# A second-matrix pair more per group by seven products, and the MLP's row factor moved onto the residual

## The reference, cut to what matters

```
y = h * rsqrt(mean(h*h) + 1e-6) * gain
h = h + square(relu(y @ w_up)) @ w_down      # w_up 1024 x 4096, w_down 4096 x 1024, float32
```

## Time and profile before

| | us |
|---|---|
| median of 3 runs (1189.15 to 1189.55) | 1189.25 |
| the profiled execution's own time | 1188.87 |
| its span, first to last instruction | 1187.1 |
| PE / PE weight load busy | 1176.7 / 1126.4 |
| DVE / ACT / POOL busy | 957.6 / 740.0 / 118.2 |
| MLP of layer 0: first matmul of the first pair to the end | 250.9 to 597.5 |
| MLP of layer 1, up to the tail | 839.9 to 1154 |

### The profile page before, as it was taken

The page is one execution under the profiler, slowest core; times in us unless marked ns, Lnnn a source line. Parts: engine busy times, 40 slices in busy tenths (PEclk is TensorE's granted clock), DMA queues, the critical chain, the costliest instruction groups (busy, mean ns, idle before and its releaser), DMA issues.

```text
span 1187.1 us, 22848 instructions
## 1 busy us (share of the span) xinstructions
PE 1176.7 (99%) x8809; PEld 1126.4 (95%) x8809; DVE 957.6 (81%) x1423; ACT 740.0 (62%) x1305; POOL 118.2 (10%) x177
## 2 busy tenths in 40 slices
PE   9999999999999999999999999999999999999998
PEld 8999999999999999999999999987798999989988
DVE  6889888787888788886568889887878888978853
ACT  6777877745556565555357887787555556656643
POOL 3211120100110110112010000000001001001000
PEclk9999999999999999999999999999999999999999
DMA  7343342432563553565232122214334636446522
GB/s 180 95 107 92 89 101 86 135 122 72 142 144 100 116 144 107 114 184 169 54 90 71 54 71 71 88 36 125 126 107 107 143 108 156 128 125 142 174 96 72
DMA packets 152470, 131.87 MB, mean 111 GB/s; under 512 B 23304, under 2 KB 143168, under 8 KB 152384
## 3 DMA queue, kind: packets, MB, share of 16 engines
q1 hardware_dynamic: 141600, 104.93, 30.7%
q0 software_dynamic: 10656, 25.66, 9.6%
q10 hardware_dynamic: 128, 0.09, 0.0%
HBM read 111.43 MB, written 19.24 MB: 110 GB/s over the span
## 4 chain that ended last, share of the span: by engine, by line
PE 79%; issue 17%; DVE 2%; ACT 1%; POOL 1%; DMA 0%; DVEq 0%; POOLq 0%; ACTq 0%
PE ps L2330 32%; PE ps L2282 21%; PE ps L2047 18%; PE ps L2549 2%; PE ps L2102 1%; PE ps L2120 1%; PE ps L2234 0%; PE ps L2199 0%; DMA meta_in<-in_meta_tokens_dram 0%; PE ps L2188 0%; ACT wh L765 0%; DVE lo L1660 0%; DVE ps L1685 0%; POOL khm L751 0%; PE ps L2063 0%
## 5 line engine op out<-in xcount | busy, mean ns | idle before, releaser
L2047 PE MATMUL ps<-yh,wh 128*128 128x264 f32 (+1 forms) x704 | 160.5, 302 | 0.0
L2047 PE MATMUL ps<-yh,wl 128*128 128x264 f32 (+1 forms) x704 | 155.3, 295 | 0.0
L2047 PE MATMUL ps<-yl,wh 128*128 128x264 f32 (+1 forms) x704 | 155.3, 294 | 0.0
L765 ACT ACTIVATE hi<-lof 128x1024 fp32r<-128x1024 f32 x80 | 82.8, 1054 | 76.8 <-DVE lof L1653 76.8
L2330 PE MATMUL ps<-th,hi 128*128 128x264 f32 (+1 forms) x448 | 127.0, 283 | 0.9 <-ACT pu L765 0.8
L1660 DVE TENSOR_TENSOR lo<-lof,hi 128x1024 fp32r<-128x1024 f32 x80 | 97.0, 1223 | 37.5 <-ACT hi L765 37.5
L2330 PE MATMUL ps<-th,lo 128*128 128x264 f32 (+1 forms) x448 | 126.5, 282 | 0.0
L2330 PE MATMUL ps<-tl,hi 128*128 128x264 f32 (+1 forms) x448 | 126.5, 282 | 0.0
L765 ACT ACTIVATE hi<-raw 128x1024 fp32r<-128x1024 f32 (+1 forms) x128 | 115.3, 915 | 12.3 <-DMA raw<-in_mlp_w_up_dram 8.2
L2282 PE MATMUL ps<-ah,hi 128*128 128x264 f32 (+1 forms) x448 | 115.6, 316 | 0.0
L2282 PE MATMUL ps<-al,hi 128*128 128x264 f32 (+1 forms) x448 | 115.6, 316 | 0.0
(11 more groups left out here) (325 smaller groups left out, 3292.2 us busy)
## 6 DMA issues: line engine op xcount, KB each, us to landing
raw<-in_mlp_w_up_dram SPq DMA_DIRECT2D x32, 1024.0 KB, 6.6
raw<-in_mlp_w_down_dram SPq DMA_DIRECT2D x32, 1024.0 KB, 5.0
raw<-in_diff_w_in_dram SPq DMA_DIRECT2D x24, 512.0 KB, 3.8
raw<-in_mlstm_w_in_dram SPq DMA_DIRECT2D x16, 512.0 KB, 4.6
h_sum<-abuf POOLq DMA_DIRECT2D x24, 264.0 KB, 6.9
h_sum<-abuf POOLq DMA_DIRECT2D x24, 256.0 KB, 7.2
h_sum<-h POOLq DMA_DIRECT2D x16, 264.0 KB, 2.5
h<-h_sum POOLq DMA_DIRECT2D x8, 528.0 KB, 6.0
```

Source lines behind the costliest of these rows:

```text
L765: return nc.scalar.activation(o, i, ACT.Copy, scale=scale)
L2047: last = mm(ps[:, bank + s, 0:w_], w[:, slot, kb, :], m[:, kb, t0:t0 + w_], start=(kb == 0 and n == 0), stop=(kb == CB - 1 and n == 2))
```

## The change

`DOWN_FROM` becomes 5, so three of four down pairs of the first three groups are crossed. PE's order, DVE's and ACT's orders around that, and the place of the row factor change with it:

- **PE order.** A run of down pairs begins A11, A12, S1, then A11 and A12 of the next pair, then S2, S4, S3, S1 of the next pair, A22; the second pair of the run then is S2, S4, S3, A11 and S1 of the third, A22.
- **Activation sums** are made in three parts (row blocks 0 and 1, then 2, then 3), twelve instructions per group in place of four. Parts 0 and 1 are made during pair 8g+3, part 2 during pair 8g+4. The low part of S3's sum moves into pair 8g+4.
- **Row factor.** `norm_factor` also writes the mean square ms (one more ACT instruction) and makes r^2 = exp(-ln(ms)). h is multiplied by ms on DVE before it is saved (`scale_residual`, after the forms of pair 2), r^2 is refined by r^2 * (2 - ms * r^2) (`refine_factor`, two DVE instructions during pair 2), the up halves go out of PSUM by an ACT Relu (`positive`) in place of DVE's max-times-r, and the last down pairs get two DVE instructions (add, then times r^2) in place of one. The save of h is four DMAs of two row blocks each in place of eight.
- The first squares (of pairs 0 and 1) wait in ACT's queue until pair 2, behind the copy P1 and behind the save of h.

The diff, cut to its core:

```diff
-DOWN_FROM = 6
+DOWN_FROM = 5
@@ pe_order
-            yield from [(i, "A11"), (i, "A12"), (i, "S1"), (i, "S2")]
+            yield from [(i, "A11"), (i, "A12"), (i, "S1")]
+            if not is_up(i):
+                yield from [(i + 1, "A11"), (i + 1, "A12")]
+            yield from [(i, "S2")]
+        elif is_up(i) or crossed(i - 2):
+            yield from [(i, "S2"), (i, "A12")]
         else:
-            yield from [(i, "S2"), (i, "A12")]
+            yield from [(i, "S2")]
         if crossed(i + 1):
-            yield from [(i, "S4"), (i, "S3"), (i + 1, "A11"), (i + 1, "S1"), (i, "A22")]
+            yield from [(i, "S4"), (i, "S3")]
+            if is_up(i) or crossed(i - 1):
+                yield from [(i + 1, "A11")]
+            yield from [(i + 1, "S1"), (i, "A22")]
@@ gpsimd: residuals
-                for k in range(CB):
-                    pool.wait_ge(h_ready, 16 * layer + k + 1)
-                    pool.dma_start(h_sum[k], h[:, k, :]).then_inc(h_saved, 16)
+                for q in range(4):
+                    pool.wait_ge(h_scaled, FACTOR * layer + q + 1)
+                    pool.dma_start(h_sum[2 * q:2 * q + 2, :, t0:T].rearrange("k p t -> p k t"),
+                                   h[:, 2 * q:2 * q + 2, t0:T]).then_inc(h_saved, 16)
@@ scalar: norm_factor
+                if n % 2:
+                    nc.scalar.activation(tokens(ab[1], spans), src, ACT.Identity, bias=eps_d[:, 0:1], scale=1.0 / D).then_inc(ms_rd, 1)
...
-                nc.scalar.activation(tokens(rb[:, :], spans), tokens(rb[:, :], spans), ACT.Exp, scale=-0.5).then_inc(rb_ready, 1)
+                nc.scalar.activation(tokens(rb[:, :], spans), tokens(rb[:, :], spans), ACT.Exp,
+                                     scale=-1.0 if n % 2 else -0.5).then_inc(rb_ready, 1)
@@ scalar: mlp
+                def positive(i, m):
...
+                    nc.scalar.activation(pair_tokens(tb[m], layer, i), pair_out(layer, i, m), ACT.Relu).then_inc(m_evac, 1)
                 def squares(i, m):
...
+                    if i > 0:
+                        positive(i, m)
...
                     if i == 0:
-                        act.wait_ge(h_saved, 16 * CB * (layer + 1))
+                        act.wait_ge(h_saved, 64 * (layer + 1))
@@ scalar: loop over the pairs
+                    if i == 1:
+                        positive(0, 1)
...
                     if begins:
                         snap(i, "P1")
-                        if is_up(i):
-                            squares(i - 1, 1)
-                        else:
+                        if i == PLAIN:
+                            squares(0, 0)
+                            squares(0, 1)
+                        if not is_up(i):
                             block_hi(i, "S3")
                         snap(i, "P5")
+                        if i == PLAIN:
+                            squares(1, 0)
                     first_down = begins and not is_up(i)
                     if crossed(i + 1) and first_down and DOWN_FROM > 5:
                         form_hi(i + 1, "S14")
                     if crossed(i) and (begins or not is_up(i)):
                         snap(i, "U2")
+                    if i == PLAIN:
+                        squares(1, 1)
                     if first_down:
                         block_hi(i, "A22")
                     if crossed(i + 1) and not (first_down and DOWN_FROM > 5):
                         form_hi(i + 1, "S14")
@@ vector: mlp
+                def scale_residual():
+                    dve.wait_ge(ms_rd, layer + 1)
+                    for q in range(4):
+                        rows = h[:, 2 * q:2 * q + 2, t_in:T]
+                        V.tensor_tensor(rows, rows, ab[1][:, t_in:T].unsqueeze(1).broadcast_to([P, 2, T - t_in]),
+                                        ALU.mult).then_inc(h_scaled, 1)
@@ vector: evacuate, last group's down pairs (the up halves' branch is gone)
-                    V.tensor_tensor(tokens(h[:, k, :], spans), src, tokens(h[:, k, :], spans), ALU.add).then_inc(m_evac, 1)
+                    V.tensor_tensor(tokens(tbuf, spans), pair_out(layer, i, m), tokens(h[:, k, :], spans), ALU.add).then_inc(row_sum, 1)
+                    dve.wait_ge(row_sum, 8 * layer + k + 1)
+                    V.tensor_tensor(h[:, k, t_in:T], tbuf[:, t_in:T], rb[:, t_in:T], ALU.mult).then_inc(m_evac, 1)
@@ vector: loop over the pairs
+                    if i < PAIRS - 8 and i % 8 == 3:
+                        block_forms(i, ("S3", "S1", "S2", "A22"), 0)
                     if crossed(i) and not (begins and not is_up(i)):
                         total(i, "C22")
...
+                    if i == PLAIN:
+                        for n in range(4):
+                            act_lo(n // 2, n % 2)
...
+                    if i < PAIRS - 8 and i % 8 == 3:
+                        block_forms(i, ("S3", "S1", "S2", "A22"), 1)
...
+                    if sent_down(i) and i % 8 == DOWN_FROM - 1:
+                        natural_lo(i + 2, True)
+                        block_forms(i, ("A22",), 2)
+                        block_lo(i, "S2")
+                        block_lo(i + 1, "S3")
...
+                    if i == PLAIN:
+                        refine_factor()
...
                         form(i + 2, "S4", 3)
+                        if i == 0:
+                            scale_residual()
```

More of the change, by code:

```diff
@@ L126 @@
         | counted(("gain_rd", "ym_made", "gwh_done", "gw_ready", "ym_lo")))
+FACTOR = 6
 N_DONE, N_READY, N_TAKEN, N_OUT, N_CROSSED, N_COPIED, N_ADDED, N_SENT = (
@@ L1044, in snap @@
                         copy(pu[:, 1, 0:w], product_bank(layer, i, "S2")).then_inc(p_copied, 1)
+                def positive(i, m):
+                    if not crossed(i):
+                        act.wait_ge(m_done, items + DONE[i, m])
+                    else:
+                        if m == 1:
+                            act.wait_ge(m_done, items + DONE[i, "A22"])
+                        act.wait_ge(c_done, adds + ADDED[i, "C22" if m else "C1"])
+                    wait(act, ah_done, 8 * (4 * layer + i // 8) + 2 * (i % 8) + m - 1)
+                    nc.scalar.activation(pair_tokens(tb[m], layer, i), pair_out(layer, i, m), ACT.Relu).then_inc(m_evac, 1)
                 def squares(i, m):
@@ L1084, in block_hi @@
                 def block_hi(i, name):
-                    act.wait_ge(b_made, 4 * ((GROUPS - 1) * layer + i // 8) + BLOCK_MADE[name])
+                    act.wait_ge(b_made, 12 * ((GROUPS - 1) * layer + i // 8) + 8 + BLOCK_MADE[name])
                     if name in ("S3", "A22"):
@@ L1136, in mlp @@
                         form_hi(i + 1, "S23")
-                    if i > 0 and not in_tail(layer, i - 1) and not sent_down(i - 1) and not (sent_down(i) and i % 8 == 4) and not begins:
+                    if i > 1 and not in_tail(layer, i - 1) and not sent_down(i - 1) and not (sent_down(i) and i % 8 == 4) and not begins:
                         finish(i - 1, 1)
@@ L1637, in mlp @@
                 items, ranks, norm = layer * N_DONE, layer * N_CROSSED, 2 * layer + 1
-                copies, adds = layer * N_COPIED, layer * N_ADDED
+                copies, adds, t_in = layer * N_COPIED, layer * N_ADDED, spans[0][0]
                 def form(i, name, after):
@@ new lines, in refine_factor @@
+                def refine_factor():
+                    made, ms, r = FACTOR * layer + 5, ab[1][:, t_in:T], rb[:, t_in:T]
+                    dve.wait_ge(rb_ready, norm + 1)
+                    V.scalar_tensor_tensor(ms, ms, -1.0, r, ALU.mult, ALU.mult).then_inc(h_scaled, 1)
+                    dve.wait_ge(h_scaled, made)
+                    V.scalar_tensor_tensor(r, ms, 2.0, r, ALU.add, ALU.mult).then_inc(h_scaled, 1)
+                    dve.wait_ge(h_scaled, made + 1)
+                def evacuate(i, m):
@@ L1763, in mlp @@
                     up_before = crossed(i - 1) and is_up(i - 1)
-                    if up_before or i > 0 and not is_up(i - 1) and not in_tail(layer, i - 1) and not sent_down(i - 1):
+                    if i > 0 and not is_up(i - 1) and not in_tail(layer, i - 1) and not sent_down(i - 1):
                         evacuate(i - 1, 1)
@@ L1768, in mlp @@
                         act_lo(i - 1, 1)
-                        block_forms(i, ("S3", "S1", "S2"))
-                    if begins and not is_up(i):
-                        block_lo(i, "S3")
+                        block_forms(i, ("S3", "S1", "S2"), 2)
                     if crossed(i + 1):
@@ L1813, in mlp @@
                     if crossed(i + 2):
-                        natural_lo(i + 2, True)
+                        if not (sent_down(i) and i % 8 == DOWN_FROM - 1):
+                            natural_lo(i + 2, True)
                         form(i + 2, "S1", 0)
```

66 lines of the change are left out of this document (25 added, 41 removed).

## The result

| | before | after | predicted |
|---|---|---|---|
| median of the runs, us | 1189.4 (4 runs) | 1206.33 (1205.83 to 1206.76, 4 runs) | 1204.5 (1192 to 1210) |
| ratio | | 1.0141, 95% interval 1.0124 to 1.0159 | |
| profiled execution: its span, us | 1187.1 | 1204.2 | |

The account below looks back on a forecast made before the run. PE, busy 99% of the span, was taken to bound the kernel. Terms -8.1 + 12.5 + 6.7 + 3.7 + 0.5 gave +15.3 on 1188.87 us, 1204.2; medians lie 0.4 higher, hence 1204.5, range 1192 to 1210.

Parts of the forecast that it names:

- Matmuls saved: One plain pair per group becomes crossed, three groups in each layer: 1.5 us each in layer 0, 1.2 in layer 1; -8.1.
- The six group starts: Pairs 13 and 14 and their like: two ACT/DVE chains outlast fewer covering products, 2.1 us in each of six groups; +12.5.
- The signs that the prediction named: In the changed profile, S1 of pair 14 starts about 3.9 us after pair 13's S4, S2 about 2.8 after A22.
- rival 3: Knock-on: late run starts delay third pairs' forms, or the save lands late; 0.7 us per group, 3 at starts; 1211.7; chance 0.12.
- The starts: Pairs 2 and 3, once per layer: h's save and the squares delay PE, 3.75 and 4.1 us less today's waits; +6.7.
- The save: At the start of layer 0's crossed up pairs, h is saved at 278.5, bounds 276.5 and 280, taking 4.5 us.
- Pair 3's A22: Once per layer: 9.4 us of DVE work precedes C22, so A22 waits 1.8 us, 1.9 in layer 1; +3.7.
- The end: The last evacuation gets a second instruction, 0.42 us and its handover; everything after it waits: +0.5 us.
- costed at nothing: Up evacuations moved from DVE to ACT, and the last group's second instructions under plain pairs with DVE idle: no cost.
- The sum: -8.1 + 12.5 + 6.7 + 3.7 + 0.5 = +15.3 us, giving a median of 1204.5.
- Rival 1: All stays hidden at S1 and S2 of pair 14 and its like, with DVE relieved: faster, 1181.6; chance 0.12.
- Rival 2: The starts are absorbed, the groups are not: save lands in time, pair 3's sums are early; 1194; chance 0.18.

Follow-up runs that it names:

- The reordered kernel: The changed kernel with ACT rounding block A22 and S14 ahead of U2, and DVE making low parts of A22, S14 and S23 ahead of C22: 1189.92 us.
- the kernel with all moves: The changed kernel with both queues reordered at group starts, scaling and squares moved at the MLP starts, pair 29's second half evacuated earlier: 1183.94 us.
- the crossing alone: The kernel before with only DOWN_FROM changed from 6 to 5: 1210.79 us, ratio 1.0175.
- six pairs: The changed kernel with DOWN_FROM back at 6 and the old order of products and natural low parts, keeping new residual and three-part sums: 1221.52 us.
- the kernel that was mended: The changed kernel with DOWN_FROM 6 and old product order, plus block S3's low part put back to the start of pair 6's DVE turn: 1201.37 us.

## Why the prediction was right, and where not

The forecast was 1204.5, the time 1206.3. By its own steps:

- **Matmuls saved, -8.1.** Confirmed at 8.2 by the difference of two traces.
- **The six group starts, +12.5.** Right in mechanism and in the three waits. Waits for S1, A22 and S2 were put at 1.0, 0.15 and 1.25; the trace has 0.99, 0.10 and 1.20, in layer 1 1.02 and 1.20. The signs that the prediction named (S1 of pair 14 3.9 us after S4 of pair 13, S2 2.8 after A22) are there: 411.19 less 407.30 is 3.89, and 415.48 less 412.75 is 2.73. (From its own waits and today's the prediction's term comes to 12.2; it rounded each group up.) As a sum the term was too small. From A11 of pair 13 to A11 of pair 16 PE needs 32.00 us for 20 products of 1.4585, so 2.8 us are lost where three named waits make 2.3; over the six groups the same count gives 17.2 us, less 2.2 before the change: 15.0 where 12.5 stood. The rest is gaps of under 0.2 us behind the late starts, a wait of 0.67 us at S2 of pair 7 and one of 0.32 at S1 of pair 23. That is the knock-on of rival 3, in small pieces. The reordered kernel lost 0.5 us in the same count.
- **The starts, +6.7.** Sizes of 0.5, 0.6, 1.2, 0.1 and 1.35 were given; they are 0.62, 0.52, 0.90, 0.12 and 1.20 in layer 0, 3.4 us where 3.75 stood. In layer 1 they are 1.04, 0.52, 0.96, 0.1 and 1.18, 3.8 where 4.1 stood. Less today's waits that is 6.1. The save was put at 278.5 and ACT's squares began at 278.69. The Trainium skill's fit for such a transfer ("DMA: Bandwidth & Descriptors", Anatomy of one DMA) gave an estimate of 3.2 us; the first of the save's four DMAs landed after 3.2 us here, as the fit says. The last, behind the other three, took 4.7 us here and 7.4 us where it was issued ten microseconds earlier, so for the one that ACT waits for the fit, which has no term for other traffic, was low in both.
- **Pair 3's A22, +3.7.** The mechanism is right, its size a quarter too large: 1.45 and 1.49 us where 1.8 and 1.9 stood. The nine microseconds of DVE's work ahead of C22 were 9.1, not 9.4.
- **The end, +0.5, and "costed at nothing".** Here a step failed. The second instructions of the last group's down pairs were said to "lie under plain pairs with DVE idle". DVE is idle there, but it waits for ACT. Evacuation, square, rounding and low part follow one another across the two engines, and each second instruction makes the turn 0.7 us longer. After two such turns 1.6 us of wait, start less start, come out at the tail's third unit; moving one evacuation took that wait away. The +0.5 itself was too large for the end of the span: PE does wait 0.5 us for the last sum, but with the evacuation moved the end comes only 0.1 us later than in the kernel before. The sum should have had +1.8 here.
- **The sum.** With what was measured it is -8.2 + 15.0 + 6.1 + 2.9 + 1.8 = 17.6, and the two profiled spans differ by 17.1; the 0.5 between them is not assigned. The prediction's +15.3 was short by the groups (2.5) and the tail (1.3), and long by the starts (1.4). So part of its closeness is luck: errors of 3.8 and 1.4 us had opposite signs.
- **Rivals.** Rival 1 (all hidden) failed, and for the reason given against it: a DVE relieved of 44 us of evacuations still stands idle ahead of the two chains. (Nor is it relieved as a whole: the change gives it other work, and its busy time rose from 957.6 to 974.5 us.) Its time of 1181.6 is nearly what the kernel with all moves reaches (1183.94), so the gain was there, but only behind a reordering that the change lacks. Rival 2 (the starts absorbed) fell with five named waits per layer. Rival 3 (knock-on) came to 2.5 us in the groups; the save was not late.

Relu on ACT cost the steady pairs nothing: with both chains in order PE had no wait over 0.15 us inside the groups of either layer. The row has 0.60 us for it, beside the 0.61 that was used.

## What to carry to other kernels

When a change takes products out of a run, ask of each in-order queue what stands ahead of the instruction that the next product needs: here 16 us hung on the place of a few instructions at each of six group starts, a place that was right for the old order of products. An engine that is idle a fifth or a third of the time is no cover if that idle time lies in front of a wait; cost an added instruction at nothing only where the chain through both engines is shorter than PE's turn. And test such a change by moving both queues at once: each queue alone gave 3 and 6 us of the 16.

## What was not expected of the hardware

In two of these kernels the granted clock of TensorE fell to half, its 1.2 GHz level, for about 3.4 us at a time. The row by windows of the kernel with the crossing alone, around S3 of pair 5 (the columns are PE, PEld, DVE, ACT, POOL, the granted clock, the share of DMA and GB/s):

```profile
317.00:318.00 1.00, 0.00 (x0) 0.00 (x0) 1.00 (x2) 0.72 (x1) 0.00 (x0) 1.00 0.99 331
318.00:319.00 1.00, 0.53 (x4) 0.53 (x5) 0.97 (x2) 1.00 (x2) 0.00 (x0) 0.98 0.77 268
319.00:322.00 3.00, 3.00 (x15) 3.00 (x15) 1.52 (x3) 1.87 (x3) 0.00 (x0) 0.50 0.13 47
```

PE had just waited 2.4 us and was at work again when the clock fell, with 15 matmuls in 3 us where 25 fit at full clock. That makes each wait cost about 1.7 us more than its length. It came after 10 of the 14 waits of 2.25 to 2.5 us in these kernels (5 of 6 with the crossing alone, 5 of 7 with six pairs, not after the one of 2.43 us in the kernel that was mended) and after none of the shorter ones in the MLPs, the longest of which was 1.9 us. Why it spared four of them is open. It explains the miss with six pairs: in the two profiled executions the crossed runs of that kernel lose 19.1 us more than those of the mended one, 11.2 of them in waits and 7.9 beside them, which is what five stretches at half clock come to; the spans differ by 18.7 and the medians by 20.2. The changed kernel had no such stretch in its MLPs.

The other surprise was the save of h: the same four DMAs landed 5.1 us after the scaling in one place and 7.8 us in another. The traces show what else the DMA engines had to do. SP issues a load of 1 MB of weights at about 259.1 in both kernels, and it takes 6.5 us. In the changed kernel the save is issued from 270.40 on, to idle DMA engines, and 0.84 MB of it have moved before 274. In the other it is issued from 260.49 to 264.00, in the middle of that load. These are its queues from 256 to 264 (packets, MB, share of the 16 engines), the load's above and the save's below, and then the times to landing of layer 0's four DMAs in the changed kernel and in the other:

```profile
q1 hardware_dynamic: 861, 0.88, 44.7%
q0 software_dynamic: 2, 0.01, 0.3%
...
DMA to landing us min/median/max: 3.2/3.9/4.7
...
DMA to landing us min/median/max: 6.5/6.8/7.4
```

Almost none of the save moved before its last issue, while the load's packets, about 1 KB each, kept the engines some nine tenths busy once they had begun. The run with only the scaling moved shows the same 6.5/6.8/7.4, with its save issued at 262.3 to 265.8. So moving a store earlier gained less than the move, most likely because it met a load there. A run with the load moved was not made, so this is read from the traces and not shown by experiment.
